# Sweeping the last four weight units of two output projections token half by token half

## The reference

```python
def rms_norm_2(x, g):
    xf = x.astype(jnp.float32)
    y = xf * lax.rsqrt(jnp.mean(xf * xf, axis=-1, keepdims=True) + EPS)
    return (y * g.astype(jnp.float32)).astype(x.dtype)
...
        x = x + cross_attn(x, mem, xa_norm[layer], xa_mem_norm[layer], xa_wq[layer],
                           xa_wk[layer], xa_wv[layer], xa_wo[layer])
        x = x + conv_ffn(x, f_norm[layer], f_w_up[layer], f_dw_w[layer], f_dw_b[layer],
                         f_w_down[layer])
    return rms_norm_2(x, final_norm)
```

## Time and profile before

| | us |
|---|---|
| median of 3 executions (1784.05 to 1786.11) | 1785.7 |
| profiled execution, device time | 1786.79 |
| profiled execution, span from first to last instruction | 1785.0 |
| PE busy in it | 1753.5 (98%) |
| DVE busy | 1184.5 (66%) |
| ACT busy | 1019.3 (57%) |

### The profile page before, as it was taken

One profiled execution on the slowest core, in us unless ns is written; L12 is line 12 of the kernel. 1 busy time (PEld: TensorE's weight loads), 2 busy tenths in 40 slices (PEclk: granted clock), 3 DMA queues, 4 the chain that ended last, 5 costly groups with the idle time before them and its releaser, 6 DMA issues.

```text
span 1785.0 us, 26657 instructions
## 1 busy us (share of the span) xinstructions
PE 1753.5 (98%) x10506; PEld 1570.4 (88%) x10506; DVE 1184.5 (66%) x1567; ACT 1019.3 (57%) x1402; POOL 121.4 (7%) x204
## 2 busy tenths in 40 slices
PE   7999999999999999999999999999999999999998
PEld 7888898888989888888889978899999988889997
DVE  5866676666757586765678666665666986466654
ACT  6965556454676655644555946654456426555444
POOL 5000000000000000000000000500003550000000
PEclk9999999999999999999999999999999999999999
DMA  9546555565655565556665653566565415345663
GB/s 306 160 155 181 176 168 155 173 190 186 213 178 165 161 181 162 167 162 190 189 207 178 186 177 119 155 188 185 184 187 178 153 48 177 117 154 184 185 188 106
DMA packets 166188, 306.75 MB, mean 172 GB/s; under 512 B 12362, under 2 KB 24564, under 8 KB 165936
## 3 DMA queue, kind: packets, MB, share of 16 engines
q1 hardware_dynamic: 163168, 298.91, 54.1%
q0 software_dynamic: 2896, 6.15, 1.1%
HBM read 303.97 MB, written 1.05 MB: 171 GB/s over the span
## 4 chain that ended last, share of the span: by engine, by line
PE 93%; DVE 3%; ACT 2%; issue 1%; DMA 1%; DVEq 0%; ACTq 0%
PE bank L1626 50%; PE bank L1644 31%; PE bank L2012 3%; PE bank L2042 2%; PE bank L1656 1%; PE bank L1930 1%; DVE h_lo L1072 1%; PE bank L1666 1%; PE bank L1674 1%; DVE weights_lo L1031 0%; DMA weights_raw<-in_w_out_dram 0%; ACT h_hi L636 0%; PE bank L1858 0%; PE bank L1823 0%; PE bank L1904 0%
## 5 line engine op out<-in xcount | busy, mean ns | idle before, releaser
L1031 DVE TENSOR_TENSOR weights_lo<-weights_raw,weights_hi 128x1024 fp32r<-128x1024 f32 x560 | 669.3, 1227 | 405.2 <-ACT weights_hi L566 402.5
L566 ACT ACTIVATE weights_hi<-weights_raw 128x1024 fp32r<-128x1024 f32 x560 | 575.4, 1056 | 417.7 <-DMA weights_raw<-in_w_in_dram 169.5
L1644 PE MATMUL bank<-h_hi,weights_hi 128*128 128x256 f32 x1376 | 391.4, 284 | 4.0 <-DVE h_lo L1072 2.5
L1644 PE MATMUL bank<-h_lo,weights_hi 128*128 128x256 f32 x1376 | 390.1, 283 | 0.0
L1644 PE MATMUL bank<-h_hi,weights_lo 128*128 128x256 f32 x1376 | 390.0, 283 | 0.0
L1626 PE MATMUL bank<-weights_hi,h_hi 128*128 128x512 f32 x928 | 364.1, 392 | 2.5 <-DVE h_lo L1085 1.6
L1626 PE MATMUL bank<-weights_hi,h_lo 128*128 128x512 f32 x928 | 361.3, 389 | 0.0
L1626 PE MATMUL bank<-weights_lo,h_hi 128*128 128x512 f32 x928 | 361.2, 389 | 0.0
L1626 PE MATMUL bank<-weights_hi,arena_parts 128*128 128x512 f32 x928 | 293.8, 392 | 3.3 <-DVE weights_lo L1031 1.8
L1644 PEld LDWEIGHTS bank<-h_hi,weights_hi 128*128 128x128 f32 x1376 | 264.8, 192 | 5.6 <-issue 2.1
L1644 PEld LDWEIGHTS bank<-h_hi,weights_lo 128*128 128x128 f32 x1376 | 264.9, 192 | 0.5
(11 more groups left out here) (316 smaller groups left out, 1658.7 us busy)
## 6 DMA issues: line engine op xcount, KB each, us to landing
weights_raw<-in_w_in_dram SPq DMA_DIRECT2D x224, 512.0 KB, 3.5
weights_raw<-in_f_w_up_dram SPq DMA_DIRECT2D x96, 512.0 KB, 3.8
weights_raw<-in_f_w_down_dram SPq DMA_DIRECT2D x48, 512.0 KB, 3.7
weights_raw<-in_w_up_dram SPq DMA_DIRECT2D x40, 512.0 KB, 3.7
weights_raw<-in_c_w_pw_dram SPq DMA_DIRECT2D x24, 512.0 KB, 3.5
weights_raw<-in_ab_w_in_dram SPq DMA_DIRECT2D x20, 512.0 KB, 3.6
weights_raw<-in_w_mem_kv_dram SPq DMA_DIRECT2D x16, 512.0 KB, 3.7
weights_raw<-in_w_out_dram SPq DMA_DIRECT2D x16, 512.0 KB, 3.7
```

The costliest lines, as they stand in the source:

```text
L566: nc.scalar.activation(w_hi[:, q % SPLIT, 0:w], raw[:, n % RAW, 0:w], ACT.Copy).then_inc(hi_done, 1)
L1031: tt(w_lo[:, n % RAW, 0:w], raw[:, n % RAW, 0:w], w_hi[:, q % SPLIT, 0:w].bitcast(F32), ALU.subtract)\
L1644: ins = mm(bs[i][:, j, :], wp[:, kk, f * P:(f + 1) * P], sp_[:, 2 * u + kk, :], start=first and u == us[0] and kk == 0 and n == 0 and j == ...
```

## The change

The last four weight units of X1's and of F1's output are now taken by a new function `proj_by_tokens`: it takes all four units for tokens 0 to 127 (n = 0 then n = 1), and then sweeps the same four for tokens 128 to 255, releasing each unit in the second sweep. Banks complete in the order (n, t) = (0,0), (1,0), (0,1), (1,1). DVE's additions follow in a new `residual_by_tokens`, ACT's squares by the changed `pieces`. The first layer's X0 and F0 keep the old code.

```diff
--- before.py
+++ after.py
@@ -263,7 +263,7 @@
 
         def pieces(prev):
 
-            return [(n, t) for t in range(NT) for n in range(2)] if prev[0] == "L" else [(n, t) for n in range(2) for t in range(NT)]
+            return [(n, t) for t in range(NT) for n in range(2)] if prev[0] == "L" or prev in ("X1", "F1") else [(n, t) for n in range(2) for t in range(NT)]
 
         def bank(C, name, i=0):
             return ps[PLACE[C.stage, name, i]]
@@ -622,7 +622,7 @@
                 log_exp_table()
                 for n, t in pieces(prev):
                     if (n, t) == (1, 1):
-                        past("o", 3, 2, prev)
+                        past("o", 3, 4 if prev in ("X1", "F1") else 2, prev)
                     act.wait_ge(vec_done, after_vec(f"res{n}{t}", prev))
                     square(xs[:, t, n * 512:(n + 1) * 512], "h", t, n)
                     if n:
@@ -1114,6 +1114,17 @@
                 link(tt(r, r, n, ALU.add))
                 link(ts(cs[:, 0], r, PI, -PI, ALU.min, ALU.max), "trig.in")
 
+            def residual_by_tokens(then):
+                for t in range(NT):
+                    for n in range(2):
+                        b = filled("o", 2 * n + t, 3 if n and not t else 4)
+                        if n:
+                            base("h", t, then)
+                        xv = xs[:, t, n * 512:(n + 1) * 512]
+                        link(tt(xv, b[:, :], xv, ALU.add), ("free", "o", 2 * n + t), f"res{n}{t}")
+                if then == "end":
+                    link(tt(rows_of(0)[:, 1, 0:W], xs[:, 1, 0:W], brow[:, D:D + W], ALU.mult), "gained")
+
             def residual(then):
                 for n, t in pieces("X"):
                     if n and not t:
@@ -1446,7 +1457,7 @@
                     low_of_bank("oT", h, h_hi[:, 2 * h:2 * h + 2, :], h_lo[:, 2 * h:2 * h + 2, :], f"oT{h}hi", f"o_lo{h}")
                 if l == 0:
                     mem_low(M_HL["X"], COL_F[1] + 8, cols2)
-                residual(f"F{l}")
+                (residual_by_tokens if l else residual)(f"F{l}")
 
             def ffn(l):
                 VC.enter(f"F{l}")
@@ -1472,7 +1483,10 @@
                              ("free", f"u{j}", i), *([f"h{j}"] if i else []))
                     dve.wait_ge(act_done, after_act(f"h{j}hi"))
                     link(tt(F_HL[j % 2][1], c, F_HL[j % 2][0].bitcast(F32), ALU.subtract), f"h{j}lo")
-                residual("C" if l == 0 else "end")
+                if l:
+                    residual_by_tokens("end")
+                else:
+                    residual("C")
 
             cross(0)
             ffn(0)
@@ -1629,6 +1643,27 @@
                         if last and u == us[-1] and t == 0:
                             end(ins, name, i0)
                     used(ins, *([(name, i0 + 1)] if last and u == us[-1] else []))
+
+            def proj_by_tokens(name, us, src, first):
+
+                bs = [begin(name, i) if first else bank(PC, name, i) for i in range(4)]
+                kept = []
+                for t in range(NT):
+                    for n in range(2):
+                        for u in us:
+                            if t == 0:
+                                kept.append((at[0], unit(2, W)))
+                            m, w = kept[n * len(us) + us.index(u)]
+                            for kk in range(2):
+                                for q, (wp, sp_) in enumerate(passes(w, src)):
+                                    ins = mm(bs[2 * n + t][:, :], sp_[:, 2 * u + kk, t * P:(t + 1) * P], wp[:, kk, :],
+                                             start=first and u == us[0] and kk == 0 and q == 0,
+                                             stop=u == us[-1] and kk == 1 and q == 2)
+                            done = [(name, 2 * n + t)] if u == us[-1] else []
+                            if done or t:
+                                ins.then_inc(pe_done, PC(*done))
+                            if t:
+                                PC.marks["unit", m] = PC.n
 
             def proj_F(name, i0=0, src=H_HL, us=ALL, first=True, last=True, ready=None):
 
@@ -1969,6 +2004,10 @@
                 values(2)
                 values(3)
                 proj_T("o", 2, us=(0, 1), last=False)
+                if l:
+                    pe.wait_ge(vec_done, VC.at("o_lo3"))
+                    proj_by_tokens("o", (2, 3), H_HL, False)
+                    return
                 for n in range(2):
                     proj_T("o", 2 * n, us=(2, 3), first=False, ready="o_lo%d")
 
@@ -1990,7 +2029,11 @@
                     proj_F(f"u{j}")
                     if j:
                         down(j - 1)
-                down(5)
+                if l:
+                    pe.wait_ge(vec_done, VC.at("h5lo"))
+                    proj_by_tokens("o", (0, 1), F_HL[1], False)
+                else:
+                    down(5)
 
             cross(0)
             ffn(0)
```

## The result

| | before | changed |
|---|---|---|
| median of 13 executions each, us | 1786.11 | 1790.33 |
| lowest to highest, us | 1784.05 to 1788.6 | 1788.5 to 1793.3 |
| span of the profiled execution, us | 1785.0 | 1786.8 |

The ratio is 1.0026, with a 95% interval of 1.0019 to 1.0034: about 4.6 us slower. That is clear of no change; the ratio lies above the 0.2% that the prediction took as the limit, but the lower end of the interval lies just under it. The measured time lies inside the predicted range, 1.8 us above its point. The profiled execution grew by only 1.8 us. The two profiles show why that number cannot be taken for the change's price.

The account below looks back on a forecast made before the run. TensorE bounds the kernel (93% of the chain), so changes count only where it waits or behind its last matmul. 2.0 in X1 plus 0.8 at the end gave +2.8 us, a median of 1788.5; range 1785.8 to 1790.8.

Parts of the forecast that it names:

- TensorE's sweep: X1 and the end: the same 48 matmuls in another order, costed at nothing.
- X1, the chain: X1's output: weight splits between additions make ACT and DVE start the last addition 2.0 us later.
- lower bound of 1.2: X1's delay if each of 14 steps behind the first addition starts 0.06 us sooner.
- upper bound of 2.5: X1's delay if TensorE's clock is low by the transposes, so that these delay the gains.
- Weight loads: Behind X1: buffers released up to 4.1 us later, over 7 us before ACT needs their refill; cost nothing.
- rival 4: Feed-forward: late weight loads collide, TensorE waits at its fifth unit; up to +2 us more, about 1790.5; chance 0.05.
- The end: Kernel end: base and gained delay the final product and first store; 0.8 us later, bounds 0.5 and 0.9.
- the drain of 2.7 us unchanged: Kernel end: the final stores' drain was to stay at 2.7 us.
- Rival 1: End and X1: first half's store leaves early (-1.3 us), low clock spared (-1.7 us); 1782.7; chance 0.07.
- The clock: Feed-forward after X1's gap: same low-clock cost as before, nothing in the sum, 1.7 us either way as bounds.
- rival 2: X1's gap: added idle keeps the clock low for longer, +1.7 us for a second low stretch; 1790.2; chance 0.25.
- My own sign for a mis-sized clock: X1's gap at 7.9 us but the total moved by under 1 us or over 4.

Follow-up runs that it names:

- splits_first: Changed kernel with all four weight splits of X1 ahead of the first addition again; 1788.36 us, ratio 1.0012 to the kernel before.
- mended: As splits_first, with base ahead of the bank wait and the first half's final product in two pieces before the last two additions; 1784.75 us, ratio 0.9995.
- end_only: Changed kernel with X1 put back as before, only the end of F1 and the final norm token by token; 1787.03 us, ratio 1.0006 to before.
- mended_later: As mended, but only three of X1's four weight units split ahead of the first addition, the fourth behind the norm; 1786.43 us, ratio 0.9999 to before.
- before_fill: Kernel before with four extra matmuls ahead of F1's transposes and three behind, into a bank nothing reads; 1786.48 us, ratio 0.9996.

## Why the prediction was right, and where it was not

- *TensorE's sweep costs nothing.* Right: the 48 matmuls start within 10.65 us of each other before and after, in X1 and at the end of F1.
- *X1, the chain, +2.0.* Right in place and mechanism, 1.84 measured (last addition 1.95 behind the last matmul instead of 0.11). splits_first removed 1.7 of it by the splits alone. From the first to the last addition it was 10.08 us, 10.12 in my list; the first came 0.08 us sooner than forecast. (My lower bound of 1.2 should have read 1.1: fourteen steps of 0.06 off 1.96.) Behind the last addition I had 5.8 us unchanged; it was 6.35 in this profile, since the clock was low by the time of the transposes. My upper bound of 2.5 had that case in view, and the gap grew by 2.41.
- *Weight loads, nothing.* Right: TensorE has no idle stretch between the first and the last matmul of F1. That answers rival 4.
- *The end, +0.8.* Right for DVE and the first store's issue (+0.82). What failed here is "the drain of 2.7 us unchanged": it took some 0.9 us more in the changed kernel, by the look of the rate through one late DMA engine. The bound of 0.9 for the whole end was too narrow; it measured 1.71. Rival 1's price for draining half of the output early, 1.3 us, was too high as well: in mended it was 0.5.
- *The clock, nothing in the sum.* This term was mis-sized for the median. The mean clock fell from 0.9977 to 0.9962. How much that is worth comes from 101 executions of the kernel before that ran beside the experiments: those with a clock of 0.999 span 1783.1 us in the mean, those with 0.996 span 1786.8, so 0.001 goes with 1.2 us and 0.0015 with 1.8. Part of it is not lost time: the low stretch over the stores counts in the clock and costs no matmul, and in the two profiles it is 6.0 us long instead of 3.8, which alone takes some 0.0006 off the mean clock. From the other side, the means of the 13 and 13 device times differ by 4.6 us, and 1.84 + 1.71 of them are accounted for (as measured in the one profile), which leaves 1.1. Between 1.1 and 1.8, then, as an estimate, since the clocks compared come from different sessions and the rest has no measurement of its own. All 13 executions of the changed kernel had a clock of 0.997 or lower, against 52 of the 101: so something of rival 2 seems to have been at work in most executions, rather than all of it in a quarter of them, as I had it.
- *The sum.* 2.8 forecast, 4.6 measured: 1.84 in X1 and 0.82 from DVE at the end, both as forecast and both tested; 0.9 from the slower drain, whose cause is open; the rest, about 1.1, put down to the clock but not isolated. My own sign for a mis-sized clock, a total of over 4 us, was met. That the time still lies in the range is in part luck: the room above the point was meant for rival 2, and a term I had not thought of, the drain, took about half of what was used of it.
- *The chances.* I gave 0.61 to a change within 0.2% and 0.35 to slower by more. By the ratio the less likely case came. Both terms that I left at nothing, the drain and the clock, came out at a cost.

The Trainium skill (TensorE: Matmul & The Clock Gate, Part 4: PE-mode transpose) had it that transposes do not count as activity the way matmuls do. The traces are in line with it, but do not prove it. In the changed kernel the clock fell in the idle stretch ahead of the transposes (at 1569.2) and stayed low through most of them, and in none of the six kernels with extra matmuls around the same transposes did it fall there. But among the eight without them it did not fall there either in end_only and mended_later, with the same gap of 5.9 us as before.

## What to carry to other kernels

When a helper decides how much background work (here the splitting of weights) is done ahead of each wait, changing the order of the waits moves that work too: print each engine's order and lay the steps end to end before believing that an earlier result starts anything earlier. Completing half of the data early can pay only if its consumer stands ahead of the last wait in the program of the engine that runs it, and even then, here, it paid 0.5 us in the profile. And for a change of a few microseconds take many executions: in one profile F1 alone can differ by 1.5 us through where the clock falls.

## What was not expected of the hardware

- A single fetch of instructions among full-rate stores goes with a tail 0.65 to 0.9 us longer (five of five profiles; the cause is not isolated). So an edit in X1 can go with a cost at the end, 200 us later, with the same instructions there.
- Executions of the same kernel spread over 4 to 5 us (1784.3 to 1789.1 in 33 of them), in step with the mean granted clock of each. In its profile the kernel before had one low stretch in F1 and one near 1034, the changed kernel one over its transposes; before_fill had none, and neither had end_only around F1, with the same X1 as before. Only the low stretch over the final stores is in all of them.
- Issuing half of the output 2 us earlier shortened the tail by 0.5 us only: from the issue of the last 256 KB store to the end of the span it was 2.7 us with 256 KB right ahead of it (mended) and 3.3 us with 768 KB (before).
